# Two modulation sums between two layers: from one f32 product each to two products of rounded type, with the rest made on GpSimd

## The chip, the cores and the metric

The kernel runs on one core of one Trainium2 chip. The metric is the device time of one execution in microseconds. Times in the trace are counted from the start of the profiled span. The engines are TensorE (PE; its weight loads are PEld), VectorE (DVE), ScalarE (ACT), GpSimd (POOL) and SyncE (SP), which issues most of the transfers.

## The reference

256 tokens of width 1024 pass through an attention block with an MLP, then through two layers whose norms are modulated by a vector `c`: layer 0 (convolutions and a recurrent unit, then SwiGLU) and layer 1 (stick-breaking attention, then SwiGLU). All of it is float32. What matters here:

```python
def ada_modulation(c, ada_w, ada_b):
    m = jax.nn.silu(c) @ ada_w + ada_b
    return jnp.split(m, N_MOD, axis=-1)          # sh_m, sc_m, g_m, sh_f, sc_f, g_f

def layer(x, c, ...):                            # both layers have this form
    sh_m, sc_m, g_m, sh_f, sc_f, g_f = ada_modulation(c, ada_w, ada_b)
    h = modulate(rms_norm_2(x, mix_norm), sh_m, sc_m)
    ...
    x = x + g_m[:, None, :] * (o @ w_out)
    hf = modulate(rms_norm_2(x, ffn_norm), sh_f, sc_f)
    return x + g_f[:, None, :] * swiglu(hf, ffn_w_gate, ffn_w_up, ffn_w_down)
```

The changed place is the end of layer 0's SwiGLU, where `g_m` of layer 1 is made ready.

## The kernel before

**Weights in two parts.** Every weight part of 128x1024 is loaded as f32 into `w_raw`, rounded by ScalarE to the type fp32r (`w_hi`, line 728) and its rest `w_raw - w_hi` made by VectorE (`w_lo`, line 1153). Activations are treated alike: `aT_hi` and `aT_lo` are the transposed operand, [128, 8 blocks, 256 tokens] each, `hT_hi` and `hT_lo` the hidden one. A product is then three products of rounded type: hi by hi, hi by lo, lo by hi.

**The modulation.** VectorE accumulates `silu(c) * ada_w` row by row into `mod`, [128, 6 x 1024], so that each partition holds a part of each sum; the count of these steps is `ada_used`. The sum over the partitions is a product with a matrix of ones that leaves the total in every partition of a PSUM bank, and ScalarE copies it back over `mod` (`ada_parts`, line 788, count `ada_out`). A function `ada_sums` does it for 512 columns with one f32 product (line 2165). Four sums of layer 0 are done in another form, `rounded_sums` (lines 2149 and 2150): ScalarE rounds 1024 columns to fp32r in one instruction (`rounded`, line 833, count `ada_hi`), VectorE subtracts to get the rest (`rounded_rest`, line 1376, count `ada_lo`), and TensorE adds ones by hi and ones by lo in one bank, for each 512 columns. `GATE_M` is `mod[:, 2048:3072]`, the columns of `g_m`.

**The place.** After the last down product of layer 0's SwiGLU, TensorE runs `ada_sums(1, 4, 6)` (line 2278), the two sums of `GATE_M` of layer 1. Then comes `entry` (line 1928), the start of layer 1's first projection: eight transposes of token tile 0 (`norm_T`, line 1896), a third sum, ten products of tile 0 with the rounded weights of parts 0 to 3 (line 1942), of which part 3 waits for its rounding by `hi_done`, two more of part 3, four with `aT_lo`, a fourth sum (it waits for `x_ready` of tile 1), the transposes of tile 1, and so on.

What stands around it in the queues, each in program order and with semaphores between them:

- VectorE, `gated_norm` (line 1295): for tile 0 gate times output and residual in two halves (lines 1274 and 1278), times gain (1167); first half of tile 1's gate (1304); times `rstd` plus shift, two halves, which makes `xn` (1178); second half of tile 1's gate, residual of tile 1 (1278), times gain (1167); then `aT_lo` of tile 0 (1161), `xn` of tile 1.
- ScalarE, `norm` (line 756): squares of tile 0 (line 738), a weight rounding, the copies of the two sums, `aT_hi` of tile 0 (777), squares of tile 1, the rounding of weight part 3, and on.
- GpSimd: `row_rstd` (line 643) takes the row sums of the squares (648) and makes `rstd` by a power (649), tile 0 and then tile 1. Before that it fills and loads the biases of layer 1's modulation (638, 639).

The blocks 0 to 3 of `aT_hi` and `aT_lo` are not in use from the last gate and up products of layer 0 until the norm writes them; blocks 4 to 7 hold one weight part there.

Of the kernel before, what the change touches and what calls it, by code (L numbers as in the profile page):

```python
# [26 lines left out]
F32 = mybir.dt.float32  # L27
F32R = mybir.dt.float32r
ALU = mybir.AluOpType
# [8 lines left out]
CH = 512  # L38
# [77 lines left out]
def block_program(nc, a, out):  # L116
    ctx = ExitStack()
    with ctx:
# [19 lines left out]
        aT_hi, aT_lo = aT[:, 0, :, :], aT[:, 1, :, :]  # L138
# [13 lines left out]
        sums = sb("sums", [P, 2])  # L152
# [99 lines left out]
        def flat(h):  # L252
            return h.rearrange("p b n -> p (b n)")
# [19 lines left out]
            return apart[v][1] if v in apart else w_lo[:, slot_of(v), :]  # L273

        hT_sums = flat(hT_hi[:, :, :]), flat(hT_lo[:, :, :])

        def ada_of(j, t):

# [345 lines left out]
        @block.gpsimd  # L624
        def _(pool):
            n_chain = [0]

            def chained(ins):

                n_chain[0] += 1  # L630
                ins.then_inc(pool_chain, 1)
                pool.wait_ge(pool_chain, n_chain[0])

            def start_sums(layer, third, dst=None):

                c = slice(third * UNIT, (third + 1) * UNIT)
                dst = mod[:, c] if dst is None else dst
                chained(pool.memset(dst, 0.0))
                pool.dma_start(dst[0:1, :], ada_b[layer][:, c]).then_inc(ada_bias, 16)

            n_rstd = [0]

            def row_rstd(tiles=(0, 1)):

                for t in tiles:
                    n_rstd[0] += 1
                    pool.wait_ge(sq_done, n_rstd[0])
                    chained(pool.tensor_scalar(var[:, t:t + 1], sums[:, t:t + 1], 1.0 / D, EPS, ALU.mult, ALU.add))
                    pool.tensor_tensor(rstd[:, t:t + 1], var[:, t:t + 1], half[:, 0:1], ALU.pow).then_inc(rstd_done, 1)

            n_half = [0]

            def half_var(t, h):

                n_half[0] += 1
                n_rstd[0] += 1
                pool.wait_ge(sq_half, n_half[0])
                pool.tensor_scalar(var[:, t:t + 1], half_sums[:, 2 * t + h:2 * t + h + 1], EPS, None,
                                   ALU.add).then_inc(var_done, 1)

            pool.memset(eps[:, :], EPS)
            pool.memset(ones[:, :], 1.0).then_inc(consts, 1)
            chained(pool.memset(half[:, :], -0.5))
            chained(pool.memset(ident[:, :], 0.0))
            chained(pool.affine_select(out=ident[:, :], in_=ident[:, :], compare_op=ALU.not_equal, fill=1.0,
                                       base=0, pattern=[[-1, P]], channel_multiplier=1))
            pool.memset(rg_w[:, :, :, :], 0.0).then_inc(consts, 1)
            n_rstd[0] += NT

            chained(pool.iota(neg_dist[:, 0:P], pattern=[[1, P]], base=0, channel_multiplier=-1,  # L670
                              allow_small_or_imprecise_dtypes=True))
            chained(pool.iota(neg_dist[:, P:SC], pattern=[[1, TOK]], base=-P, channel_multiplier=-1,
                              allow_small_or_imprecise_dtypes=True))
            chained(pool.memset(sb_mask[:, :], 0.0))
            pool.affine_select(out=sb_mask[:, :], in_=sb_mask[:, :], compare_op=ALU.is_ge, fill=NEG, base=-1,
                               pattern=[[-1, P]], channel_multiplier=1).then_inc(consts, 1)
            for lo, n, q0 in ((0, P, 0), (P, TOK, P)):
                part = neg_dist[:, lo:lo + n]
                pool.affine_select(out=part, in_=part, compare_op=ALU.is_ge, fill=NEG, base=q0,
                                   pattern=[[-1, n]], channel_multiplier=1).then_inc(consts, 1)  # L680
            for step, n in ATT_STEPS:
                if step == "E" and n < 3:
                    start_sums(0, n)
            pool.wait_ge(o_ready, HEADS)
            pool.wait_ge(mix_used, 11)
            start_sums(1, 0, mod_next)
            half_var(0, 0)
            half_var(1, 0)
            half_var(0, 0)
            half_var(1, 0)  # L690
            half_var(0, 0)
            half_var(0, 0)
            half_var(1, 1)
            half_var(1, 0)
            row_rstd()
            pool.wait_ge(xn_done, 16)
            start_sums(1, 1)
            start_sums(1, 2)
            row_rstd()
            pool.wait_ge(ada_gain_done, 3)  # L700
            chained(pool.memset(stick_new, 0.0))
            for last in (P - 1, SC - 1, SC + P - 1):
                pool.memset(stick_new[:, last:last + 1], 1.0).then_inc(new_sticks, 1)
            row_rstd()
# [3 lines left out]
        def _(act):  # L708
# [47 lines left out]
            def norm(u, layer=None, parts=(0, 0, 0, 0)):  # L756

                k = n_norm[0]
                n_norm[0] += 1
                ada_parts(layer, parts[0], parts[1])  # L760
                for t in range(NT):
                    act.wait_ge(x_ready, 2 * (k - 1) + t + 1)
                    row_square(t, x[:, t, :])
                    if k == 4 or t == 1:
                        split_part(2 * u + 2 + t)
                    ada_parts(layer, parts[1 + t], parts[2 + t])
                    if t == 0:
                        norm_hi(k, 0)
                    if t == 0 and k in (3, 5):
                        split_part(2 * u + 2)  # L770
                norm_hi(k, 1)
# [272 lines left out]
            def swiglu(layer):  # L1044
                u, j0, g0 = SG_U[layer], H0[layer], S0[layer]

                def hi(j, i=None):
                    act.wait_ge(h_ready, plus(j0 + j + 1, i, 2))
                    act.activation(hT_hi[:, hT_blocks(j), :], sg_h, ACT.Copy).then_inc(hT_hi_done, 1)

                def first():

                    split_hi(u + 2)
                    act.wait_ge(w_used, parts_to(u + 2))
                    act.activation(sg_silu, tp[:, :, 0:TOK], ACT.Silu).then_inc(act_h, 1)
                    split_hi(u + 3)
                    act.wait_ge(h_T, 2 + layer)
                    act.activation(hT_hi[:, hT_blocks(0), :], blocks_in(acc[:, 0:1, :])[:, 0],
                                   ACT.Copy).then_inc(hT_hi_done, 1)

                def one(v, j, i=None):

                    if j >= 2:
                        split_part(2 * v + 3, i, 6)
                    split_part(2 * v + 4, i, 6)
                    act.wait_ge(w_used, parts_to(v + 1, i, 6))
                    act.wait_ge(act_h, plus(j0 + j, i, 2))
                    act.activation(sg_gate, ub[:, :, TOK:], ACT.Copy).then_inc(g_rest, 1)
                    split_part(2 * v + 5, i, 6)
                    act.wait_ge(g_sum, plus(g0 + j, i, 2))  # L1070
                    act.wait_ge(h_ready, plus(j0 + j, i, 2))
                    act.activation(sg_silu, sg_gate, ACT.Silu).then_inc(act_h, 1)
                    split_part(2 * v + 6, i, 6)
                    act.wait_ge(w_used, parts_to(v + 2, i, 6))
                    act.activation(sg_up, tp[:, :, TOK:], ACT.Copy).then_inc(u_rest, 1)
                    split_part(2 * v + 7, i, 6)
                    hi(j, i)
                    if i is None and j == NJ_SG - 1:
                        return
                    split_part(2 * v + 8, i, 6)  # L1080

                first()
                one(u + 2, 1)
                with act.Fori(0, (NJ_SG - 3) // 2) as i:
                    for q in range(2):
                        one(u + 5 + 3 * q, 2 + q, i)
                one(u + 3 * NJ_SG - 4, NJ_SG - 1)
                split_hi(u + 3 * NJ_SG)

            swiglu(0)  # L1090
            norm(U_QKV2, 1, (4, 4, 6, 8))

            act.wait_ge(small_loaded, 16 * 8)
# [43 lines left out]
        def _(dve):  # L1137
# [566 lines left out]
                split_lo(u + 3 * NJ_SG)  # L1704

            swiglu(0)
            dve.wait_ge(ada_gain_done, 3)
            gated_norm(3, U_QKV2, gate_ffn, G_M, SH_M)
            ada_gain(1, 4, 20)
# [68 lines left out]
        def _(pe):  # L1778
# [373 lines left out]
            def blocks_of_bank(bank, n):  # L2152
                return bank.rearrange("p (b n) -> p b n", n=n)

            def hT_halves():
                return [[part[:, i * CH:(i + 1) * CH] for i in range(2)] for part in hT_sums]

            def ada_sums(layer, n0, n1):

# [114 lines left out]
                down(u + 3 * NJ_SG - 1, (NJ_SG - 1) % 2, lo_count=j0 + NJ_SG, final=True, left=last_left)  # L2274

            swiglu(0)
            pe.wait_ge(ada_used, 40)
            ada_sums(1, 4, 6)

            def last_sum():  # L2280
                pe.wait_ge(x_ready, 8)
# [98 lines left out]
```

## Time and profile before

| what | us |
|---|---|
| median of 3 runs | 898.9 (898.3 to 899.69) |
| the profiled execution, its own time | 898.97 |
| its span in the trace | 896.9 |
| PE busy | 887.0 (99%) |
| DVE busy | 694.5 (77%) |
| ACT busy | 501.3 (56%) |
| POOL busy | 28.9 (3%) |

The page gives busy time by engine, the chain of work that ended last, and the costliest groups. The timelines list an engine's instructions in order of time, like ones merged, with the idle time before them and what ended it in brackets. The ends of matmuls are modelled: they overlap the next one, so what an instruction takes from the queue is the distance from one start to the next. The profiled execution's own time is 2.07 us more than its span.

### The profile page before, as it was taken

Reading aid. Unit: us, or ns where it says so; the run is one execution under the profiler, and the core shown is the slowest. Engines: PE = TensorE matmul, PEld = TensorE weight load, DVE = VectorE, ACT = ScalarE, POOL = GpSimd, SP = SyncE. Lnnn points to the kernel's source line nnn. Section 1 sums busy time; section 2 is a strip of 40 time slices with the busy share of each in tenths; the row PEclk is TensorE's granted clock in tenths of the full one; section 3 lists DMA queues with packets and bytes.
Section 4 is the critical chain, followed back from the end, with each engine's and each line's share of the span. In section 5 each row is a group of like instructions: output and inputs, shape, how many; then the busy total and the mean of one; then the engine's idle time right before and its main releaser. Section 6 shows DMA issues by size and latency. Waiting matters only on the chain.

```text
span 896.9 us, 13257 instructions
## 1 busy us (share of the span) xinstructions
PE 887.0 (99%) x4833; PEld 749.7 (84%) x4833; DVE 694.5 (77%) x733; ACT 501.3 (56%) x672; POOL 28.9 (3%) x52
## 2 busy tenths in 40 slices
PE   8999999999999999999999999999999999999998
PEld 5998878888888799979888888878777888888886
DVE  4698977998888986996888888686796765655655
ACT  5545675555556758755455455465675465545542
POOL 4000110000000100011000000010000000000000
PEclk9999999999999999999999999999999999999999
DMA  6989586899989375546988888636435366666661
GB/s 219 341 268 350 174 291 205 322 361 354 338 325 329 116 267 179 181 158 205 360 302 319 318 298 282 194 111 211 137 100 150 108 207 192 188 187 187 187 190 67
DMA packets 117091, 208.04 MB, mean 232 GB/s; under 512 B 7236, under 2 KB 81068, under 8 KB 111928
## 3 DMA queue, kind: packets, MB, share of 16 engines
q1 hardware_dynamic: 116566, 205.31, 68.1%
q10 hardware_dynamic: 290, 2.10, 0.7%
q8 instruction: 28, 0.46, 0.2%
q14 instruction: 15, 0.12, 0.0%
q0 software_dynamic: 192, 0.05, 0.0%
HBM read 206.39 MB, written 1.05 MB: 231 GB/s over the span
## 4 chain that ended last, share of the span: by engine, by line
PE 87%; DVE 7%; DMA 2%; ACT 2%; issue 1%; SPq 0%; DVEq 0%; ACTq 0%
PE ub L1923 11%; PE tp L1923 10%; PE acc L1824 7%; PE acc L1825 7%; PE acc L1827 7%; PE ub L1924 5%; PE tp L1924 5%; PE acc L1787 4%; PE acc L1788 4%; PE acc L1789 4%; PE acc L1942 4%; PE tp L1942 3%; PE acc L1910 3%; PE acc L1912 3%; PE acc L1911 3%; DVE w_lo L1153 2%
## 5 line engine op out<-in xcount | busy, mean ns | idle before, releaser
L1153 DVE TENSOR_TENSOR w_lo<-w_raw,w_hi 128x1024 fp32r<-128x1024 f32 x283 | 341.9, 1222 | 109.2 <-ACT w_hi L728 108.7
L728 ACT ACTIVATE w_hi<-w_raw 128x1024 fp32r<-128x1024 f32 x283 | 296.5, 1057 | 216.3 <-PE acc L1827 50.1
L1923 PE MATMUL tp<-aT,w_hi 128*128 128x512 f32 x432 | 153.9, 399 | 0.0
L1923 PE MATMUL ub<-aT,w_hi 128*128 128x512 f32 x432 | 153.6, 398 | 0.0
L1924 PE MATMUL tp<-aT,w_lo 128*128 128x256 f32 x432 | 121.3, 281 | 0.0
L1924 PE MATMUL ub<-aT,w_lo 128*128 128x256 f32 x432 | 121.2, 281 | 0.0
L1824 PE MATMUL acc<-w_hi,hT_hi 128*128 128x512 f32 x284 | 111.5, 393 | 0.7 <-DVE w_lo L1153 0.7
L1825 PE MATMUL acc<-w_lo,hT_hi 128*128 128x512 f32 x284 | 110.6, 390 | 0.0
L1827 PE MATMUL acc<-w_hi,hT_lo 128*128 128x512 f32 x272 | 106.2, 391 | 0.0
L1923 PEld LDWEIGHTS tp<-aT,w_hi 128*128 128x128 f32 x432 | 81.2, 188 | 20.0
L1923 PEld LDWEIGHTS ub<-aT,w_hi 128*128 128x128 f32 x432 | 81.2, 188 | 19.8
L1924 PEld LDWEIGHTS ub<-aT,w_lo 128*128 128x128 f32 x432 | 81.6, 189 | 1.0
L1924 PEld LDWEIGHTS tp<-aT,w_lo 128*128 128x128 f32 x432 | 81.6, 189 | 0.0
L1787 PE MATMUL acc<-w_hi,aT 128*128 128x512 f32 x160 | 64.4, 402 | 0.2 <-DVE aT L1161 0.2
L1824 PEld LDWEIGHTS acc<-w_hi,hT_hi 128*128 128x128 f32 x284 | 53.3, 188 | 12.6 <-DVE w_lo L1153 0.7
L1789 PE MATMUL acc<-w_hi,aT 128*128 128x512 f32 x160 | 62.4, 390 | 0.0
L1788 PE MATMUL acc<-w_lo,aT 128*128 128x512 f32 x160 | 62.4, 390 | 0.0
L1825 PEld LDWEIGHTS acc<-w_lo,hT_hi 128*128 128x128 f32 x284 | 53.4, 188 | 10.4
L1827 PEld LDWEIGHTS acc<-w_hi,hT_lo 128*128 128x128 f32 x272 | 51.0, 188 | 11.4
L1356 DVE SCALAR_TENSOR_TENSOR mod<-ada_raw,silu_c,mod 128x2048 f32<-128x2048 f32 x24 | 56.3, 2345 | 0.2 <-DVE mod L1356 0.2
L1910 PE MATMUL acc<-aT,w_hi 128*128 128x256 f32 x192 | 55.3, 288 | 0.0
L1912 PE MATMUL acc<-aT,w_lo 128*128 128x256 f32 x192 | 54.3, 283 | 0.0
(318 smaller groups left out, 1306.4 us busy)
## 6 DMA issues: line engine op xcount, KB each, us to landing
ada_raw<-in_l_ada_w SPq DMA_DIRECT2D x24, 1024.0 KB, 6.3
w_raw<-in_l_ffn_w_gate SPq DMA_DIRECT2D x44, 512.0 KB, 4.7
w_raw<-in_l_ffn_w_up SPq DMA_DIRECT2D x44, 512.0 KB, 3.8
w_raw<-in_l_ffn_w_down SPq DMA_DIRECT2D x44, 512.0 KB, 3.5
w_raw<-in_w_up SPq DMA_DIRECT2D x32, 512.0 KB, 4.9
w_raw<-in_w_down SPq DMA_DIRECT2D x32, 512.0 KB, 5.7
scratch<-in_l_ada_w SPq DMA_DIRECT2D x14, 1024.0 KB, 7.9
w_raw<-in_attn_w_qkv SPq DMA_DIRECT2D x24, 512.0 KB, 6.2
```

The lines of the kernel that those rows point to most:

```text
L728: act.activation(rounded_part(v), w_raw[:, v % SLOTS, :], ACT.Copy).then_inc(hi_done, 1)
L1153: dve.tensor_tensor(rest_part(v), w_raw[:, v % SLOTS, :], rounded_part(v).bitcast(F32), ALU.subtract).then_inc(lo_done, 1)
L1787: pe.matmul(outp, op_hi[:, k + n, q], wh[:, c], start=start and n == 0, stop=False)
L1788: pe.matmul(outp, op_hi[:, k + n, q], wl[:, c], start=False, stop=False)
L1789: last = pe.matmul(outp, op_lo[:, k + n, q], wh[:, c], start=False, stop=stop and n == 1)
L1824: pe.matmul(outp, operand[0][:, k, q], wh[:, c], start=start, stop=False)
L1825: last = pe.matmul(outp, operand[0][:, k, q], wl[:, c], start=False, stop=False)
L1827: last = pe.matmul(outp, operand[1][:, k, q], wh[:, c], start=False, stop=stop)
L1910: pe.matmul(outp, wh, aT_hi[:, b, :], start=b == 0, stop=False)
L1912: last = pe.matmul(outp, wl, aT_hi[:, b, :], start=False, stop=b == KB - 1)
L1923: pe.matmul(banks[f], rounded_part(v)[:, c], aT[:, :, b, :], start=b == 0, stop=False)
L1924: last = pe.matmul(banks[f][:, 0:TOK], rest_part(v)[:, c], aT_hi[:, b, :], start=False, stop=b == KB - 1)
```

## The change

The two sums of `GATE_M` of layer 1 take the second form. ScalarE rounds `GATE_M` into the blocks 0 to 3 of `aT_hi`, after the last weight rounding of the SwiGLU and ahead of the squares of the next norm; it waits for `ada_used` at 40, which TensorE waited for before. GpSimd, and not VectorE, subtracts for the rest, into the blocks 0 to 3 of `aT_lo`; in its queue that stands between the fills and `row_rstd`. TensorE runs `rounded_sums(16, ...)` in place of `ada_sums(1, 4, 6)` and waits for `ada_lo` at 3. VectorE's part only counts on in the program text. The sums go to the same two banks and are copied by the same instructions.

```diff
@@ -273,6 +273,7 @@
         hT_sums = flat(hT_hi[:, :, :]), flat(hT_lo[:, :, :])
+        aT_sums = flat(aT_hi[:, 0:4, :]), flat(aT_lo[:, 0:4, :])
@@ -696,6 +697,8 @@
             pool.wait_ge(xn_done, 16)
             start_sums(1, 1)
             start_sums(1, 2)
+            pool.wait_ge(ada_hi, 3)
+            pool.tensor_tensor(aT_sums[1], GATE_M, aT_sums[0].bitcast(F32), ALU.subtract).then_inc(ada_lo, 1)
             row_rstd()
@@ -1088,6 +1091,8 @@
             swiglu(0)
+            act.wait_ge(ada_used, 40)
+            rounded(aT_sums, GATE_M)
             norm(U_QKV2, 1, (4, 4, 6, 8))
@@ -1704,6 +1709,7 @@
             swiglu(0)
+            n_rests[0] += 1
             dve.wait_ge(ada_gain_done, 3)
@@ -2152,8 +2158,8 @@
-            def hT_halves():
-                return [[part[:, i * CH:(i + 1) * CH] for i in range(2)] for part in hT_sums]
+            def hT_halves(sums=hT_sums):
+                return [[part[:, i * CH:(i + 1) * CH] for i in range(2)] for part in sums]
@@ -2274,8 +2280,8 @@
             swiglu(0)
-            pe.wait_ge(ada_used, 40)
-            ada_sums(1, 4, 6)
+            pe.wait_ge(ada_out, 16)
+            rounded_sums(16, hT_halves(aT_sums), 3)
```

How the instructions stand on TensorE at the end of the last down product of layer 0 (line 1842) and the start of the entry; a row is a line of the kernel, the operation with the tiles it writes and reads, and what it waits for. First before, then after; the lines of the changed kernel lie a few further on (1896 is 1902, 2165 is 2171, 1942 is 1948):

```order
L1842 MATMUL acc<-aT,hT_lo 128x512
L2165 MATMUL ub<-mod,ones 128x512 [waits ada_out,ada_used]
L2165 MATMUL ub<-mod,ones 128x512 [waits ada_out]
L1896 MATMUL tp<-ident,xn 128x128 [waits xn_done]
L1896 MATMUL tp<-ident,xn 128x128 x3
L1896 MATMUL tp<-ident,xn 128x128 [waits xn_done]
L1896 MATMUL tp<-ident,xn 128x128 x3
L2165 MATMUL acc<-mod,ones 128x512 [waits tile1_gated]
L1942 MATMUL acc<-w_hi,aT 128x512 [waits hi_done,n_hi]
```

```order
L1848 MATMUL acc<-aT,hT_lo 128x512
L2155 MATMUL ub<-aT,ones_r 128x512 [waits ada_lo,ada_out]
L2156 MATMUL ub<-aT,ones_r 128x512
L2155 MATMUL ub<-aT,ones_r 128x512
L2156 MATMUL ub<-aT,ones_r 128x512
L1902 MATMUL tp<-ident,xn 128x128 [waits xn_done]
L1902 MATMUL tp<-ident,xn 128x128 x3
L1902 MATMUL tp<-ident,xn 128x128 [waits xn_done]
L1902 MATMUL tp<-ident,xn 128x128 x3
L2171 MATMUL acc<-mod,ones 128x512 [waits tile1_gated]
L1948 MATMUL acc<-w_hi,aT 128x512 [waits hi_done,n_hi]
```

Two f32 products became four of rounded type, and the wait is for the rests; all behind them stands as before.

GpSimd's queue from the fills of layer 1's biases (638) to the `rstd` of tile 0 of the norm at the changed place, before and after:

```order
L648 TENSOR_SCALAR var<-sums 128x1 [waits sq_done]
L649 TENSOR_TENSOR rstd<-var,half 128x1 [waits pool_chain]
L638 MEMSET mod 128x2048 [waits xn_done]
L639 DMA mod<-in_l_ada_b 1x16x128 [waits pool_chain]
L638 MEMSET mod 128x2048
L639 DMA mod<-in_l_ada_b 1x16x128 [waits pool_chain]
L648 TENSOR_SCALAR var<-sums 128x1 [waits sq_done]
L649 TENSOR_TENSOR rstd<-var,half 128x1 [waits pool_chain]
```

```order
L639 MEMSET mod 128x2048 [waits xn_done]
L640 DMA mod<-in_l_ada_b 1x16x128 [waits pool_chain]
L639 MEMSET mod 128x2048
L640 DMA mod<-in_l_ada_b 1x16x128 [waits pool_chain]
L701 TENSOR_TENSOR aT<-mod,aT 128x1024 [waits ada_hi]
L649 TENSOR_SCALAR var<-sums 128x1 [waits sq_done]
L650 TENSOR_TENSOR rstd<-var,half 128x1 [waits pool_chain]
```

The subtraction (701) stands ahead of the `rstd`, and waits for ScalarE's rounding.

ScalarE's queue from the last hidden rounding of the SwiGLU (1049) to the copies of the two sums (788), before and after:

```order
L1049 ACTIVATE hT_hi<-scratch 128x512 [waits h_ready]
L728 ACTIVATE w_hi<-w_raw 128x1024 [waits w_used,w_loaded2]
L728 ACTIVATE w_hi<-w_raw 128x1024 [waits w_used,w_loaded3]
L738 ACTIVATE scratch,sums<-x 128x1024 [waits x_ready]
L728 ACTIVATE w_hi<-w_raw 128x1024 [waits w_used,w_loaded0]
L788 ACTIVATE mod<-ub 128x512 [waits ada_sum] x2
```

```order
L1052 ACTIVATE hT_hi<-scratch 128x512 [waits h_ready]
L731 ACTIVATE w_hi<-w_raw 128x1024 [waits w_used,w_loaded2]
L731 ACTIVATE w_hi<-w_raw 128x1024 [waits w_used,w_loaded3]
L836 ACTIVATE aT<-mod 128x1024 [waits ada_used]
L741 ACTIVATE scratch,sums<-x 128x1024 [waits x_ready]
L731 ACTIVATE w_hi<-w_raw 128x1024 [waits w_used,w_loaded0]
L791 ACTIVATE mod<-ub 128x512 [waits ada_sum] x2
```

The rounding (836) stands between the weight roundings and the squares of tile 0.

## Rows read from the trace of the kernel before

**Rows 1.** The page, part 1: busy us, share of the span, instructions.

```profile
PE 887.0 (99%) x4833; PEld 749.7 (84%) x4833; DVE 694.5 (77%) x733; ACT 501.3 (56%) x672; POOL 28.9 (3%) x52
```

**Rows 2.** Chain that ended last, 584 to 594 us: start, length, what.

```profile
584.71 1.72 PE ub L2165 x4
```

**Rows 3.** Timeline of PE, 584.2 to 592.9: start, us, line, operation, count.

```profile
584.55 1.88 PE L2165 MATMUL ub<-mod,ones 128*128 128x512 f32 x4
586.27 1.04 PE L1896 MATMUL tp<-ident,xn 128*128 128x128 f32 x8
587.14 1.02 PE L2165 MATMUL acc<-mod,ones 128*128 128x512 f32 x2
...
592.80 0.27 PE L1896 MATMUL ub<-ident,xn 128*128 128x128 f32 x1
```

**Rows 4.** Timeline of PE at the rounded sums of layer 0, from 344.1.

```profile
344.20 0.39 PE L2149 MATMUL tp<-hT_hi,ones_r 128*128 128x512 f32 x1
...
344.89 0.39 PE L2150 MATMUL tp<-hT_lo,ones_r 128*128 128x512 f32 x1
```

**Rows 5.** Timeline of ACT, 576 to 594.

```profile
576.64 2.01 ACT L728 ACTIVATE w_hi<-w_raw 128x1024 fp32r<-128x1024 f32 x2
582.78 1.07 ACT L738 ACTIVATE scratch<-x 128x1024 f32<-128x1024 f32 x1 [4.14 <-DVE x L1278]
583.76 0.18 ACT L738 ACTIVATION_READ_ACCUMULATOR scratch<-x 128x1 f32 x1
...
588.22 1.07 ACT L738 ACTIVATE scratch<-x 128x1024 f32<-128x1024 f32 x1 [0.18 <-DVE x L1278]
...
589.28 1.05 ACT L728 ACTIVATE w_hi<-w_raw 128x1024 fp32r<-128x1024 f32 x1
```

**Rows 6.** Timeline of PE's weight loads, 584.2 to 593.

```profile
590.45 1.23 PEld L1942 LDWEIGHTS acc<-w_hi,aT 128*128 128x128 f32 x6 [0.43 <-issue]
```

**Rows 7.** Timeline of DVE, 577 to 594.

```profile
577.74 2.36 DVE L1153 TENSOR_TENSOR w_lo<-w_raw,w_hi 128x1024 fp32r<-128x1024 f32 x2 [0.15 <-ACT w_hi L728]
...
580.73 0.69 DVE L1278 TENSOR_TENSOR x<-x,xn 128x512 f32<-128x512 f32 x1
...
582.06 0.69 DVE L1278 TENSOR_TENSOR x<-x,xn 128x512 f32<-128x512 f32 x1
582.78 1.22 DVE L1167 TENSOR_TENSOR xn<-x,mod 128x1024 f32<-128x1024 f32 x1
...
584.91 1.41 DVE L1178 SCALAR_TENSOR_TENSOR xn<-xn,rstd,mod 128x512 f32<-128x512 f32 x2 [0.17 <-POOL rstd L649]
...
586.96 1.23 DVE L1278 TENSOR_TENSOR x<-x,xn 128x1024 f32<-128x1024 f32 x1
```

**Rows 8.** Timeline of POOL, 400 to 592.

```profile
404.25 1.83 POOL L638 MEMSET mod<- 128x2048 f32 x1
...
584.04 0.19 POOL L648 TENSOR_SCALAR var<-sums 128x1 f32<-128x1 f32 x1 [177.17 <-ACT scratch L738]
584.31 0.57 POOL L649 TENSOR_TENSOR rstd<-var,half 128x1 f32<-128x1 f32 x1
```

**Rows 9.** Single lines 833 and 1376: duration ns min/median/max, first and last start.

```profile
L833 ACT ACTIVATE hT_hi<-mod x2: 1042/1058/1073, 340.1 to 345.4; 128x1024 fp32r<-128x1024 f32 x2
...
L1376 DVE TENSOR_TENSOR hT_lo<-mod,hT_hi x2: 1219/1222/1226, 341.6 to 346.5; 128x1024 fp32r<-128x1024 f32 x2
```

**Rows 10.** Groups of POOL by shape: count, busy us, mean ns, idle before.

```profile
L679 POOL TENSOR_SCALAR_AFFINE_SELECT neg_dist<-neg_dist 128x256 f32<-128x256 f32 x1 | 0.4, 404 | 0.0
...
L679 POOL TENSOR_SCALAR_AFFINE_SELECT neg_dist<-neg_dist 128x128 f32<-128x128 f32 x1 | 0.3, 291 | 0.0
```

**Rows 11.** Line 658 alone, durations as in rows 9.

```profile
L658 POOL TENSOR_SCALAR var<-half_sums x8: 209/522/2227, 111.2 to 308.1; 128x1 f32<-128x1 f32 x8
```

**Rows 12.** Line 1153 alone, durations as in rows 9.

```profile
L1153 DVE TENSOR_TENSOR w_lo<-w_raw,w_hi x283: 1211/1221/1228, 7.4 to 884.0; 128x1024 fp32r<-128x1024 f32 x142
```

## The prediction

> **What bounds the kernel now.** I read the page first: TensorE (PE) is busy 99% of the span [rows 1], so the first question of any edit is what it takes from TensorE's queue. Then the chain that ended last, in the ten microseconds after layer 0's last down product: it puts the two sums that the change rewrites on the chain, with 1.72 us [rows 2]. Read alone, that row promises the whole of what the sums get cheaper. But the chain only names the engine that was busy; it does not say how far that engine could have moved. So I read, engine by engine, the timelines of the stretch from 577 to 593 us, looking for the places where TensorE meets the others.
>
> There are two. The transposes of tile 0 need `xn`, whose first half VectorE finishes at about 585.66 (half of the pair that starts at 584.91), its second at 586.32 [rows 7]; TensorE comes to them at 586.27 [rows 3], so there it is TensorE that is late. The second place is behind the first ten products of the entry: TensorE's weight load stands at 590.45 after 0.43 us idle [rows 6], put down to "issue". What this product waits for by the code is `hi_done` of part 3 of the weights: ScalarE's rounding that starts at 589.28 and ends at 590.33 [rows 5]. That rounding stands in ScalarE's queue behind the squares of tile 1 (588.22), and these behind VectorE's residual sum of tile 1, which ends at 588.19 (586.96 + 1.23) [rows 5, 7]. So at 590.45 the end is set by the queue of VectorE and not by TensorE, however busy TensorE reads. From 577.74 to that point VectorE's queue has one hole, of 0.17 us before 584.91, and that is a wait for GpSimd's `rstd`, which itself follows from VectorE's own x of tile 0 (582.75) by way of ScalarE and GpSimd [rows 5, 7, 8].
>
> **The change, part by part.** *TensorE.* Removed: two f32 sums of 512 columns. They show as 4 instructions in 1.88 us with the last one's tail; the next instruction starts 586.27 - 584.55 = 1.72 us after the first, 0.43 each [rows 3]. Added: four products of rounded type, the very form that runs for another pair of sums at 344 us: (344.89 - 344.20) / 3 = 0.23 us apart, so 0.92 us [rows 4]. Saving on TensorE: 0.80 us, and they would be through at 585.47.
>
> How much of it gets anywhere: the first four transposes then wait for `xn`, 585.66, and the last four for 586.32. The transposes take 0.87 (587.14 to 586.27) [rows 3], the second four 0.44; with some 0.1 us from a semaphore to a start (0.10 from ScalarE's 583.94 to GpSimd's 584.04 [rows 5, 8]) they end at about 586.9 instead of 587.14. TensorE is then some 0.25 us ahead, with ten products to come before the one at 590.45, and that one is held until ScalarE's 590.33. The lead goes into a longer wait there (0.28 us of real hold now, about 0.5 then). Nothing behind that point moves: the third and fourth sums, the transposes of tile 1 at 592.80 and all that follows keep their places. **Worth of the saving: 0.** If a hole opened in that second wait, at most 0.25 us would pass, and 0.80 us if both did.
>
> *ScalarE.* Added: one rounding of 128x1024, 1.06 us by the same helper's rows [rows 9]. It stands behind the two weight roundings that end at 578.65, and ScalarE is idle from there for 4.14 us, until 582.78 [rows 5]. It ends at 579.71. Its wait, `ada_used` at 40, was met in the loop long before. Queued behind it are only the squares of tile 0 (582.78), so it costs 0; were the cover gone it would cost its 1.06.
>
> *VectorE.* Nothing is added; the line there counts in the program text and issues nothing. *SyncE.* No transfer is added or moved.
>
> *GpSimd.* Added: one subtraction of 128x1024 with two operands from SBUF, from about 579.81. The trace has no such instruction on GpSimd. From below: VectorE does the same in 1.22 us [rows 9]. On GpSimd itself, a pass with one operand costs 291 ns at 128 columns and 404 at 256 [rows 10], so 0.88 ns a column and 0.18 fixed; two operands one after the other make 0.18 + 2 x 0.90 = 1.98 us. From above: the first use of a kind of instruction there took 2227 ns where the shortest of its kind took 209 [rows 11]; 2.02 more makes 4.00. I take 1.98, the row of the same engine: it ends at 581.8 (581.0 to 583.8 over the bounds). The Trainium skill (GPSIMD Engine Reference, section 3.1) has 4497 ns for a `tensor_tensor` of 2048 columns; an estimate of half gives 2.25 us and an end at 582.1, and the sum would be the same.
>
> Two things wait for GpSimd. Behind the subtraction in its queue stands `row_rstd` of tile 0 at 584.04 [rows 8], for which VectorE waits with no slack; and TensorE's sums at 584.55 now wait for `ada_lo`. The slack is 584.04 - 581.80 = 2.24 us, and 0.24 even at the upper bound. So a cost of 0.
>
> The sum: 898.97 (the profiled execution, 0.07 above the median of 898.9) - 0 + 0 = 899.0 us.
>
> **The rivals.** *The two engines get in each other's way.* While GpSimd streams from SBUF, VectorE runs subtractions and additions that also read two SBUF operands: 0.3 us of the last weight rest (to 580.10), the sum at 580.73 (0.69), later the sum at 582.06 and the gain product at 582.78 [rows 7]. VectorE's queue is the one without slack, so what it loses goes into the end one for one. If these run at half speed while GpSimd works, that is 0.30 + 0.69 = 1.0 us later. If GpSimd gives way instead, it gets only the pieces between them, 580.10 to 580.73 and 581.42 to 582.06, 1.27 us, is then shut out until 584.01, ends 0.71 us later at 584.7, and `row_rstd` is late by 0.7. Either way +0.7 to +1.0, about 899.8. For it: both read. Against it: GpSimd's fills of 1.83 us at 404.25 [rows 8] ran across weight rests of VectorE, and all 283 of these lie between 1211 and 1228 ns [rows 12]; but a fill reads nothing. The Trainium skill (GPSIMD Engine Reference, section 8, Key points) says that GpSimd shares its SBUF interfaces with VectorE and collides with VectorE instructions that have two SBUF inputs, which is this rival; no run here shows it for reads.
>
> *GpSimd is late, and the kernel slower.* This is the end on the other side: the subtraction lasts past 584.04, so longer than 4.24 us, and from there each microsecond delays `row_rstd`, `xn` of tile 0 and the whole queue of VectorE by one. It takes a first use that costs more than the 2.02 us seen and shut-out time together: 4.00 + (584.01 - 580.10 - 1.27) = 6.6 us, an end at 586.4, +2.4 us or 901.4. Against it: the short `TENSOR_TENSOR` of `rstd` has run before for the norm of layer 0, so part of the code was used.
>
> *The saving passes.* If the hold at 590.45 is not ScalarE's rounding, 0.25 to 0.80 us arrive, 898.2 to 898.7. Against it: the rounding's end and the hold match to 0.12 us, and the next product needs it by the code.
>
> *The edit doesn't do what it says*, for instance since the sums wait for their rests: then it is 899.0 as well, since TensorE's slack until 590.33 takes up a wait of up to some 1 us (0.80 + 0.28).
>
> **How the numbers follow.** Hidden, no gain (with the last case): 0.52, 899.0. Collision of the engines: 0.33, 899.8. Saving passes: 0.07, 898.5. GpSimd late: 0.08, 901.4. The likeliest case gives 899.0. The range reaches down to the full 0.80 and the spread of the runs before, 897.9, and up to the collision at its dearest plus the same spread, 900.9; it leaves out most of the late GpSimd. A measurement of this kernel tells about 0.2% (1.8 us) from no change. No mechanism of the saving reaches that (0.80 is 0.09%), so faster is only scatter, 0.03; slower is the late GpSimd and the far tail of the collision, 0.10; within, 0.87.
>
> **What the profile after would show.** Right: four products of 0.23 us in place of the sums, transposes of tile 0 up to 0.5 us earlier, a longer hold before the product at 590.45, and the transposes of tile 1 at 592.8 as before; the subtraction on GpSimd ended before 583.8; VectorE's 580.73, 582.06 and 582.78 at 0.69, 0.69 and 1.22. A collision would show as longer ones of these, or as a subtraction over 2.5 us and `row_rstd` after 584.04. Wrong altogether: transposes of tile 1 clearly before 592.8 relative to the last down product.

## The result, and the profile after

The kernel with the change takes 900.09 us (median of 20 runs, 899.36 to 901.01); the kernel before, run beside it, 898.86 us (20 runs, 898.20 to 899.98). The ratio is 1.0013 with a 95% interval of 1.0007 to 1.0019. That is 1.23 us more: inside the range, and within the 0.2% that was called "no change". But the interval does not hold 1, so the kernel is slower by a little over 0.1%, and the likeliest case of the prediction, "hidden, no gain", is not what happened.

Part 1 of the page after answers to [rows 1]:

```profile
PE 887.1 (99%) x4833; PEld 750.8 (84%) x4833; DVE 695.9 (77%) x733; ACT 502.5 (56%) x673; POOL 31.6 (4%) x53
```

The number of TensorE's instructions is the same (the profile showed each f32 product as two), its busy time too. VectorE has the same 733 instructions and is 1.4 us busier: an engine to which nothing was given. That is the first sign of the cause. ScalarE has its one rounding more, GpSimd one instruction of 2.7 us.

The timeline of VectorE after, over the last weight rests, the gated sums of tile 0 and the norm, answers to [rows 7] (start, us, line, operation, count). The profiled run of after reaches this stretch 0.67 us later (578.41 against 577.74 for the same pair of weight rests), from its start on; so durations and distances are to be compared, not starts:

```profile
578.41 2.36 DVE L1158 TENSOR_TENSOR w_lo<-w_raw,w_hi 128x1024 fp32r<-128x1024 f32 x2 [0.15 <-ACT w_hi L731]
580.68 0.68 DVE L1279 TENSOR_TENSOR xn<-acc,gate_ffn 128x512 f32<-128x512 f32 x1
581.40 2.17 DVE L1283 TENSOR_TENSOR x<-x,xn 128x512 f32<-128x512 f32 x1
583.50 0.68 DVE L1279 TENSOR_TENSOR xn<-acc,gate_ffn 128x512 f32<-128x512 f32 x1
584.21 0.69 DVE L1283 TENSOR_TENSOR x<-x,xn 128x512 f32<-128x512 f32 x1
584.94 1.22 DVE L1172 TENSOR_TENSOR xn<-x,mod 128x1024 f32<-128x1024 f32 x1
587.05 1.41 DVE L1183 SCALAR_TENSOR_TENSOR xn<-xn,rstd,mod 128x512 f32<-128x512 f32 x2 [0.17 <-POOL rstd L650]
```

GpSimd's timeline there, as [rows 8]:

```profile
580.36 2.67 POOL L701 TENSOR_TENSOR aT<-mod,aT 128x1024 fp32r<-128x1024 f32 x1 [172.83 <-ACT aT L836]
586.18 0.18 POOL L649 TENSOR_SCALAR var<-sums 128x1 f32<-128x1 f32 x1 [3.16 <-ACT scratch L741]
```

Read the two together. One VectorE row is out of line: the sum `x<-x,xn` at 581.40 takes 2.17 us where the same instruction took 0.69 [rows 7] and takes 0.69 again at 584.21. It is VectorE's first instruction with two SBUF operands after the weight rests. The weight rests end at 578.41 + 2.36 = 580.77, GpSimd's subtraction at 580.36 + 2.67 = 583.03, and the long sum at 583.57, so 0.54 after GpSimd. The product at 580.68, whose one operand is in PSUM (`acc`), takes 0.68 in the midst of it. So the rows read as if the sum did not run slowly but stood until GpSimd was through, and then ran; and as if GpSimd in its turn got going only when the weight rest had ended, so that 583.03 - 580.77 = 2.26 us of its 2.67 are work. Both readings are put to the test below (e4, e5). This is the rival "the two engines get in each other's way", in a harsher form than either of the two that I priced. The Trainium skill (GPSIMD Engine Reference, section 8, Key points) names a contention of GpSimd with VectorE instructions of two SBUF inputs; these rows agree. It also gives 4497 ns for a `tensor_tensor` add of 2048 columns (section 3.1); half of that, 2.25 us, is an estimate for 1024 columns, and the 2.26 agrees.

ScalarE and TensorE, as [rows 5] and [rows 3]:

```profile
579.23 1.04 ACT L836 ACTIVATE aT<-mod 128x1024 fp32r<-128x1024 f32 x1
584.93 1.06 ACT L741 ACTIVATE scratch<-x 128x1024 f32<-128x1024 f32 x1 [4.66 <-DVE x L1283]
```

```profile
585.22 0.40 PE L2155 MATMUL ub<-aT,ones_r 128*128 128x512 f32 x1
585.46 0.40 PE L2156 MATMUL ub<-aT,ones_r 128*128 128x512 f32 x1
585.69 0.39 PE L2155 MATMUL ub<-aT,ones_r 128*128 128x512 f32 x1
585.92 0.40 PE L2156 MATMUL ub<-aT,ones_r 128*128 128x512 f32 x1
587.86 1.32 PE L1902 MATMUL tp<-ident,xn 128*128 128x128 f32 x8 [1.54 <-DVE xn L1183]
```

The rounding is hidden with 4.66 us of idle time behind it, and the four products run 0.23 us apart. But TensorE then waits 1.54 us for the late `xn`, where before it came to the transposes without waiting.

The chain of waits over the same place shows the cause as well, if one looks for a number that is too large rather than for a new name. GpSimd's subtraction is not on it:

```profile
580.68 0.69 DVE xn L1279
581.38 0.02 issue
581.40 2.17 DVE x L1283
```

A measure of the place that does not depend on the start of the run: from the start of the last pair of weight rests to the first transpose of tile 1 ("the site"), and from there to the end of the span. It serves for all that follows.

| kernel | site, us | behind it, us |
|---|---|---|
| before | 15.07 | 304.10 |
| after | 16.52 | 303.79 |

The site is 1.45 us longer, and behind it 0.31 us are gained; the net of 1.14 stands against 1.23 between the medians. Each site below is read from one profiled run, but it repeats well: e1, e4 and e10, in which nothing is held up there, show 15.04 to 15.05, and e2 the 16.52 of after.

### The profile page after: what moved, and what is told of

Read it like the earlier page. It is cut to its first block, busy times and chain, and to the rows that moved or that the text cites. A ratio compares the mean times of both kernels' runs of the same rounds, so it can differ in the third digit from the quotient of the medians.

```text
span 898.7 us, 13259 instructions
## 1 busy us (share of the span) xinstructions
PE 887.1 (99%) x4833; PEld 750.8 (84%) x4833; DVE 695.9 (77%) x733; ACT 502.5 (56%) x673; POOL 31.6 (4%) x53
## 4 chain that ended last, share of the span: by engine, by line
PE 90%; DVE 6%; issue 2%; ACT 1%; DMA 1%; SPq 0%; POOL 0%; DVEq 0%; ACTq 0%
PE ub L1929 11%; PE tp L1929 10%; PE acc L1830 7%; PE acc L1831 7%; PE acc L1833 7%; PE ub L1930 5%; PE tp L1930 5%; PE acc L1793 5%; PE acc L1795 5%; PE acc L1794 5%; PE acc L1948 4%; PE tp L1948 3%; PE acc L1916 3%; PE acc L1918 3%; PE acc L1917 3%
```

## The experiments

The theory after the result: TensorE's saving is taken up by the hold as forecast, and the whole loss is GpSimd's subtraction, which holds up VectorE's instructions with two SBUF operands. The rivals: the sums' new form or TensorE's new wait costs it; VectorE runs at half speed; or anything at all that is added at this place costs the same.

**e1: the sums without the subtraction.** This kernel leaves the rests out of the computation.

```diff
-            pool.wait_ge(ada_hi, 3)
-            pool.tensor_tensor(aT_sums[1], GATE_M, aT_sums[0].bitcast(F32), ALU.subtract).then_inc(ada_lo, 1)
...
-                pe.wait_ge(ada_lo, n)
+                pe.wait_ge(ada_hi if n == 3 else ada_lo, n)
```

> The change without the subtraction on GpSimd: TensorE takes the second product of each sum from what aT_lo held before, so the sums miss their rests (that part of the computation is left out); everything else as in the changed kernel. Measured at the site as the time from the start of the two weight rests of VectorE (577.74 before) to the first transpose of tile 1 (592.80 before): 15.07 us before, 16.52 after. Theory (GpSimd's subtraction locks VectorE out, and the saving on TensorE is absorbed by the hold for ScalarE's weight rounding): 15.07, and the kernel at 1.0000 of before. Rival (the saving passes in part): 14.3 to 14.8, and 0.9991 to 0.9997. Rival (the loss comes from the new products or from ScalarE's rounding): stays near 16.5.

Measured: 898.36 against 898.76 (ratio 0.9996, 0.9987 to 1.0005), site 15.05 us. VectorE's sum is back at 0.69. The weight load behind the first ten products shows where TensorE's 0.80 us went:

```profile
585.17 0.42 PEld L1900 LDWEIGHTS tp<-ident,xn 128*128 128x128 f32 x4 [0.50 <-DVE xn L1181]
...
589.90 1.23 PEld L1946 LDWEIGHTS acc<-w_hi,aT 128*128 128x128 f32 x6 [0.68 <-issue]
```

About 0.5 us are lost again at the transposes, which wait for `xn`: from the first of the sums to the third sum TensorE takes 2.32 us, before 2.59. So 0.27 of the 0.80 are left behind them, and the hold grows from 0.43 [rows 6] to 0.68, by the 0.25 us of the prediction. The whole change without GpSimd's line is worth 0 at this place, as forecast.

**e2: the roundings and the subtraction, but f32 sums.**

```diff
-            pe.wait_ge(ada_out, 16)
-            rounded_sums(16, hT_halves(aT_sums), 3)
+            pe.wait_ge(ada_lo, 3)
+            ada_sums(1, 4, 6)
```

> The two f32 sums of before, with ScalarE's rounding and GpSimd's subtraction of the change kept, though nothing uses their results. Theory (the whole loss is the subtraction on GpSimd at this place): VectorE's first residual sum takes about 2.2 us in place of 0.69, the site 16.5 us, the kernel 1.0013 of before like the changed one. TensorE's transposes of tile 0 wait for xn, so the dearer sums cost nothing. Rival (part of the loss is from the sums of rounded type): clearly under 16.5.

Measured: 900.23 against 898.76 (1.0016, 1.0007 to 1.0025), site 16.52 us as in after.

```profile
580.47 2.17 DVE L1283 TENSOR_TENSOR x<-x,xn 128x512 f32<-128x512 f32 x1
```

So the loss needs nothing of the new sums. With e1, which keeps ScalarE's rounding and is not slower, this leaves only the subtraction.

**e3: the same subtraction on VectorE.**

```diff
-            pool.wait_ge(ada_hi, 3)
-            pool.tensor_tensor(aT_sums[1], GATE_M, aT_sums[0].bitcast(F32), ALU.subtract).then_inc(ada_lo, 1)
...
             swiglu(0)
-            n_rests[0] += 1
+            rounded_rest(aT_sums, GATE_M)
```

> The change with the rest made by VectorE, behind its two weight rests and ahead of the first gate product. Theory (VectorE's queue sets the end here, one for one): the instruction occupies 1.13 to 1.22 us of it, the site is 16.2 us, the kernel about 1.0012 of before, a little better than with GpSimd, though GpSimd was to relieve VectorE. Rival (VectorE has slack here): the site stays at 15.07.

Measured: 899.42 against 898.76 (1.0007, 0.9998 to 1.0016), site 16.19 us.

```profile
580.06 1.22 DVE L1379 TENSOR_TENSOR aT<-mod,aT 128x1024 fp32r<-128x1024 f32 x1
581.20 0.68 DVE L1277 TENSOR_TENSOR xn<-acc,gate_ffn 128x512 f32<-128x512 f32 x1
```

VectorE is 1.14 us later by doing the work itself, and 1.48 us later by "leaving it to GpSimd". At this place the slower engine costs more than it spares: 0.33 us more at the site. The medians alone do not settle that, since the intervals of the two kernels overlap.

**e4: GpSimd's subtraction, some 18 us earlier.** It runs in the SwiGLU of layer 0, where VectorE has gaps. ScalarE rounds into free columns of `scratch`, and GpSimd writes the rest into others beside them. Later ScalarE rounds `GATE_M` again into `aT_hi` and copies the rest into `aT_lo`, and TensorE waits for `ada_hi` at 5 (that line is not shown).

```diff
+                if layer == 0:
+                    act.wait_ge(ada_used, 40)
+                    act.activation(early[0].bitcast(F32R), GATE_M, ACT.Copy).then_inc(ada_hi, 1)
                 one(u + 3 * NJ_SG - 4, NJ_SG - 1)
...
-            act.wait_ge(ada_used, 40)
             rounded(aT_sums, GATE_M)
+            act.wait_ge(ada_lo, 3)
+            act.activation(aT_sums[1], early[1], ACT.Copy).then_inc(ada_hi, 1)
...
-            pool.tensor_tensor(aT_sums[1], GATE_M, aT_sums[0].bitcast(F32), ALU.subtract).then_inc(ada_lo, 1)
+            pool.tensor_tensor(early[1], GATE_M, early[0], ALU.subtract).then_inc(ada_lo, 1)
```

> The subtraction stays on GpSimd, with the same columns and operands from SBUF, but some 20 us earlier, at the start of the last slice of layer 0's SwiGLU (from about 562 us), where VectorE waits for ScalarE for 1.5 us between weight rests; ScalarE rounds there into scratch, GpSimd writes the rest to scratch, and ScalarE brings both into aT in its idle time before the norm. TensorE's sums are those of the change. Theory (what costs is where it runs against VectorE's queue): one weight rest of VectorE or the hole takes it, TensorE waits for nothing, the site is 15.07, the kernel 1.0000 of before (0.9997 to 1.0003). Rival (work on GpSimd, or the sums, cost wherever they stand): 1.0010 or more.

Measured: 898.73 against 898.76 (0.9998, 0.9989 to 1.0008), site 15.05 us. VectorE and GpSimd in the SwiGLU:

```profile
560.43 1.23 DVE L1163 TENSOR_TENSOR w_lo<-w_raw,w_hi 128x1024 fp32r<-128x1024 f32 x1
563.21 1.80 DVE L1163 TENSOR_TENSOR w_lo<-w_raw,w_hi 128x1024 fp32r<-128x1024 f32 x1 [1.55 <-ACT w_hi L732]
566.02 1.23 DVE L1163 TENSOR_TENSOR w_lo<-w_raw,w_hi 128x1024 fp32r<-128x1024 f32 x1 [1.01 <-ACT w_hi L732]
```

```profile
561.43 2.49 POOL L702 TENSOR_TENSOR scratch<-mod,scratch 128x1024 f32<-128x1024 f32 x1 [155.01 <-ACT scratch L1093]
```

The collision is there too, on another line of VectorE and with other tiles, so it hangs neither on one address nor on a semaphore of the changed place. And it follows from the same reading: GpSimd waits for the weight rest that ends at 561.66 and works 2.26 us until 563.92, the same 2.26 although its record is 2.49 long and not 2.67; the rest at 563.21 takes 1.80 instead of 1.22. But of the gap of 1.58 us that stands behind this rest in the kernel before, 1.01 are left, so nobody is late. The same operation costs 1.45 us in a queue without slack and 0 in one with it.

**e5: half of the subtraction (512 columns).** The other half of the rests is left out.

```diff
-            pool.tensor_tensor(aT_sums[1], GATE_M, aT_sums[0].bitcast(F32), ALU.subtract).then_inc(ada_lo, 1)
+            pool.tensor_tensor(aT_sums[1][:, 0:CH], GATE_M[:, 0:CH], aT_sums[0][:, 0:CH].bitcast(F32), ALU.subtract).then_inc(ada_lo, 1)
```

> The change with GpSimd's subtraction cut to its first 512 columns; the rests of the other 512 are left out. So far the subtraction of 1024 columns held VectorE's instruction with two SBUF operands from the end of VectorE's second weight rest until its own end, 2.26 us. Theory (GpSimd holds the way to SBUF for its whole length, in proportion to its columns): it works for 1.13 us, VectorE's first residual sum takes about 1.05 us in place of 2.17 (0.69 undisturbed), the site (from the weight rests to tile 1's transposes) is 15.4 us against 15.07 before and 16.52 after. Rival (a fixed price of the first collision): the residual sum stays near 2.2 and the site near 16.5. Rival (both at half speed, as the prediction had it): the residual sum takes about 1.2 and the second weight rest is longer than 1.22 us.

Measured: site 15.42 us (one run of 899.78 against 898.95).

```profile
578.38 2.36 DVE L1158 TENSOR_TENSOR w_lo<-w_raw,w_hi 128x1024 fp32r<-128x1024 f32 x2 [0.16 <-ACT w_hi L731]
...
581.38 1.07 DVE L1283 TENSOR_TENSOR x<-x,xn 128x512 f32<-128x512 f32 x1
```

```profile
580.33 1.57 POOL L701 TENSOR_TENSOR aT<-mod,aT 128x512 fp32r<-128x512 f32 x1 [172.84 <-ACT aT L836]
```

From the end of the weight rests (580.74) to GpSimd's end (581.90) are 1.16 us, half of 2.26; the sum ends 0.55 after that. The pair of weight rests takes 2.36 us although GpSimd waits beside it for 0.4 us: an instruction that is under way is not slowed. Both speak for "one at a time", against half speed and against a fixed price of the collision.

**e6: two instructions with one operand each in place of the subtraction.** The rests are left out here as well.

```diff
-            pool.tensor_tensor(aT_sums[1], GATE_M, aT_sums[0].bitcast(F32), ALU.subtract).then_inc(ada_lo, 1)
+            pool.tensor_scalar(scratch[:, 8192:9216], GATE_M, 0.0, None, ALU.add)
+            pool.tensor_scalar(aT_sums[1], GATE_M, 0.0, None, ALU.mult).then_inc(ada_lo, 1)
```

> The change with GpSimd's subtraction replaced by two instructions with one SBUF operand each, GATE_M plus 0 into an idle part of scratch and GATE_M times 0 into aT_lo, 1024 columns each, so the rests are left out. The prediction priced one such pass at some 1.08 us, so GpSimd works for about 2 us at the same place. Theory A (only a second SBUF operand on either side collides; one operand on GpSimd goes by): VectorE's residual sum stays 0.69 us and the site 15.07. Theory B (any reading of SBUF by GpSimd holds VectorE's instructions with two SBUF operands): the residual sum takes up to 1.8 us and the site up to 16.2.

Measured: site 16.63 us (one run of 900.46 against 898.95).

```profile
580.73 0.81 DVE L1284 TENSOR_TENSOR x<-x,xn 128x512 f32<-128x512 f32 x1
581.46 0.68 DVE L1280 TENSOR_TENSOR xn<-acc,gate_ffn 128x512 f32<-128x512 f32 x1
582.17 0.69 DVE L1284 TENSOR_TENSOR x<-x,xn 128x512 f32<-128x512 f32 x1
582.90 1.94 DVE L1173 TENSOR_TENSOR xn<-x,mod 128x1024 f32<-128x1024 f32 x1
```

```profile
579.69 3.06 POOL L701 TENSOR_SCALAR scratch<-mod 128x1024 f32<-128x1024 f32 x1 [172.85 <-ACT aT L837]
582.71 2.81 POOL L702 TENSOR_SCALAR aT<-mod 128x1024 fp32r<-128x1024 f32 x1
585.60 0.19 POOL L649 TENSOR_SCALAR var<-sums 128x1 f32<-128x1 f32 x1
```

Neither theory got this. The one-operand form is no quicker than the subtraction, 2.81 to 3.06 us, where from [rows 10] I had estimated about 1.08. And it holds VectorE only in its beginning: the sum at 580.73 loses 0.12, the one at 582.17 nothing although GpSimd's first instruction runs on to 582.75, the product at 582.90 loses 0.72. Counted from VectorE's weight rests (to 580.09) and from GpSimd's second start (582.71), both holds are over after some 0.9 to 1.0 us, by an estimate that lets the held instruction end 0.54 us after the hold for 512 columns, as in after and e5, and 1.09 for 1024, as in e4. The site's +1.56 is about 0.12 + 0.72 + 0.73, the last because `row_rstd` now starts at 585.60, behind GpSimd's own work. The second instruction's length is no slip of the profile: TensorE's first sum waited for it and started at 585.66. If GpSimd waited here too for the VectorE instruction under way, 0.40 us to 580.09 and 0.15 us to 582.86, then both instructions worked 2.66 us. Why they take so long, and why they hold VectorE in their beginning only, stays open; "GpSimd holds VectorE for its whole length" is shown for the subtraction alone.

**e8: a kernel in which the saving gets through.** The hold at [rows 6] depends on VectorE's queue, so I put the subtraction early as in e4, but on VectorE, and moved VectorE's weight rest of part 1 from before the gated sums to behind tile 1's residual sum, with tile 0's `norm_lo` next to it.

```diff
+                if layer == 0:
+                    dve.wait_ge(ada_hi, 3)
+                    dve.tensor_tensor(early[1], GATE_M, early[0], ALU.subtract).then_inc(ada_lo, 1)
                 one(u + 3 * NJ_SG - 4, NJ_SG - 1)
-                split_lo(u + 3 * NJ_SG)
+                if layer == 0:
+                    split_part(2 * (u + 3 * NJ_SG))
+                else:
+                    split_lo(u + 3 * NJ_SG)
...
                 add_gated(1).then_inc(x_ready, 1)
-                dve.wait_ge(x_ready, 2 * n + 2)
-                norm_scale(1, g)
+                split_part(2 * u_end + 1)
                 norm_lo(0, 0)
                 norm_lo(0, 1)
+                dve.wait_ge(x_ready, 2 * n + 2)
+                norm_scale(1, g)
```

> A version that is to beat both. The rest is made early, by VectorE, in its idle 1.5 us between weight rests at about 562 us (rounded into scratch by ScalarE, brought into aT by ScalarE before the norm); and VectorE's queue at the site is shortened where the end hangs on it: the rest of weight part 1 goes from ahead of the first gate product to behind the residual of tile 1, and there the two aT_lo halves of tile 0 go ahead of the gain product of tile 1. Measured from the start of the last down product (584.32 before) to the first transpose of tile 1 (592.80): 8.49 us before, 9.94 after. Theory (the cheaper sums pay only once VectorE's queue is not the limit): 7.7 us, that is 0.8 less than before, the kernel 0.9991 of before. Rival (something else holds the transposes of tile 1): 8.2 or more.

Measured: 897.89 us (897.26 to 898.59) against 898.95; ratio 0.9987, 0.9978 to 0.9996. That is about 0.1% faster than the kernel before; it was not run beside the kernel after, whose ratio to before is 1.0013. From the last down product to the first transpose of tile 1 it takes 7.82 us, before 8.49 and after 9.94.

```profile
586.14 0.68 DVE L1282 TENSOR_TENSOR xn<-acc,gate_ffn 128x512 f32<-128x512 f32 x1
586.86 1.22 DVE L1286 TENSOR_TENSOR x<-x,xn 128x1024 f32<-128x1024 f32 x1
588.00 1.22 DVE L1161 TENSOR_TENSOR w_lo<-w_raw,w_hi 128x1024 fp32r<-128x1024 f32 x1
```

```profile
589.33 0.30 PEld L1958 LDWEIGHTS acc<-w_lo,aT 128*128 128x128 f32 x2 [0.46 <-issue]
...
590.33 1.21 PEld L1958 LDWEIGHTS acc<-w_hi,aT 128*128 128x128 f32 x6 [0.25 <-issue]
```

The hold of [rows 6] has shrunk to 0.25 us, but a new one of 0.46 us stands in front of it. By the code this load waits for the rest of weight part 1, the very instruction that was moved: it ends at 588.00 + 1.22 = 589.22, and the load starts at 589.33. That is why the place takes 7.82 us and not the 7.7 expected.

Of the 1.06 us between the medians, 0.67 us come from the place (8.49 to 7.82). Another 0.32 us lie behind it (303.78 us against 304.10); they come with any added instruction on ScalarE, as e10 shows, and are no merit of the new order.

**e9: the same order of VectorE with the f32 sums of before.** Its edit is the lines of e8 on `split_part`, `norm_lo` and `norm_scale` alone, in the kernel before.

> The kernel before with the new order of VectorE's queue alone, and its two f32 sums. Theory (TensorE then runs without the hold before the product of part 3, but carries the dear sums): only the hold of 0.28 us is gained, 8.2 us from the last down product to the first transpose of tile 1, the kernel 0.9997 of before. The distance to the version with the cheap sums, 0.4 to 0.5 us, is what the change's idea is worth once the queue is moved. Rival (the new order alone brings it all): 7.7 us.

Measured: 898.46 against 898.95 (0.9994, 0.9985 to 1.0003), 8.20 us at the place. The interval holds 1, so the split of e8's gain rests on the two places in the traces: 0.29 us is the order (8.49 to 8.20), and 0.38 us (8.20 to 7.82) the sums of rounded type. So half of TensorE's 0.80 us passes with the new order, and none did with the old. The other half goes mostly to the moved rest: in e9 TensorE, coming later, did not wait for it, and the four products with `w_lo` took 0.91 us; in e8 they take 1.21, and the eight behind them another 0.08 more than in e9.

**e10: one more instruction on ScalarE, of one column, in the kernel before.** This asks for the 0.31 us that after gains behind the site.

```diff
             swiglu(0)
+            act.activation(scratch[:, 8192:8193], eps[:, 0:1], ACT.Copy)
             norm(U_QKV2, 1, (4, 4, 6, 8))
```

> The kernel before with one more instruction on ScalarE, a copy of one column into an idle part of scratch, where the changed kernel has its rounding; nothing reads it. In the profiles so far the time from the first transpose of tile 1 to the end of the span is 304.1 us in the kernel before and in the new order with f32 sums, and 303.8 in all others, and the 0.3 us lie on ScalarE at 693 us, between a wait that is over and the weight rounding behind it (0.33 us against 0.06). Theory (where ScalarE's instructions stand in its stream decides: those two kernels are the only ones without an added instruction on ScalarE): site 15.07 as before, 303.8 behind it, the kernel about 0.9997 of before. Rival (the 0.3 us belong to something else, such as the sums): 304.1.

Measured: behind the site 303.76 us, as in after (303.79), and the site itself 15.04; the time, 898.54 against 898.49 (0.9999, 0.9989 to 1.0008), can't resolve it. The 0.3 us go at one spot, a pair of roundings on ScalarE after a wait; first in the kernel before, then in e10:

```profile
693.49 2.01 ACT L728 ACTIVATE w_hi<-w_raw 128x1024 fp32r<-128x1024 f32 x2 [1.94 <-PE acc L1789]
```

```profile
693.54 2.01 ACT L728 ACTIVATE w_hi<-w_raw 128x1024 fp32r<-128x1024 f32 x2 [1.66 <-PE acc L1790]
```

The wait is 1.94 us before and 1.66 with one instruction more. It is 1.66 in every kernel here that has an added instruction on ScalarE, after among them, and 1.94 in the two that have none, before and e9. So these 0.3 us come with the added instruction and not from anything that the change computes; by what way is not shown.

## Why the prediction was right and wrong, step by step

*TensorE saves 0.80 us, and it is worth nothing.* Right, in size and in place. The products ran 0.23 us apart; e1 showed about 0.5 us going into the wait for `xn` and 0.25 into the hold. The chain [rows 2] had promised a gain of which nothing arrived, and the timelines were right. e8 and e9 confirm it from the other side: with VectorE's order changed, 0.38 us get through. One term stands in the prediction without its working, the 0.28 us of "real hold"; e9, which has no hold there, gained 0.29.

*ScalarE's rounding is hidden.* Right: 1.04 us, with 4.66 us of idle time behind it.

*GpSimd's subtraction takes 1.98 us and costs 0.* This is the step that failed, in two terms. The length, forecast at 1.98 us, was 2.26 us of work (2.67 with the wait for VectorE's weight rest). The row of one operand at 128 and 256 columns [rows 10] was not a sound base for it, as e6 showed later: there one operand of 1024 columns took 2.81 us or more, not 1.08. But 2.26 lay within the bounds of 1.22 and 4.00, and the slack to `row_rstd` covered it: that instruction followed from VectorE's x and never waited for GpSimd. The failure is the 0: I asked only who waits for GpSimd's *result*, and took the slack of those. The one who waits while it works is VectorE, with the next instruction that has two SBUF operands, and VectorE had no slack.

*The chances.* The collision stood among the rivals with 0.33, and "hidden", with 0.52, ahead of it; what happened is the rival. The row against it, the fills of 1.83 us beside undisturbed weight rests [rows 8, 12], was true and no evidence: I had noted myself that a fill reads nothing, and yet let it count.

*The collision's price.* I had 0.7 (GpSimd gives way) and 1.0 (both at half speed). It is neither: whoever has begun finishes, the other stands. VectorE then lost GpSimd's whole 2.26 us less what it could do in the meantime with an operand from PSUM, the product that ended at 581.36. The held sum has its start at 581.40. That leaves 583.03 - 581.40 = 1.63 us of standing, of which 2.17 - 0.69 = 1.48 us shows as a longer sum (it ends 0.54 us after the hold and not 0.69, as if its start had been done by then), and 1.45 us at the site. The rival named the right pair of engines and instructions; its dearest price, 1.0 us, was too small by half a microsecond.

*The sum.* 899.0 was forecast, 900.09 measured. The difference of 1.1 us is +1.45 for the missed term and -0.31 for ScalarE behind the site, which I had not foreseen and which is not owed to the sums.

*The range.* That 900.09 lies inside it is no merit of the likeliest case: the upper end, 900.9, was made for the collision. Some of it is luck, too. The collision cost more than its dearest forecast, and the 0.31 us that nobody foresaw took a part back. The two ends were also not made with "the same spread" as the text says: 898.97 - 0.80 leaves 0.27 us down to 897.9, while 898.97 + 1.0 leaves 0.93 us up to 900.9. With 0.27 on both sides the top would have been 900.2, and the result still inside, by 0.15 us.

## What to carry to other kernels

Before giving an idle GpSimd work with two SBUF operands, look at VectorE's queue at that time and not only at GpSimd's own slack: here the next instruction of VectorE with two SBUF operands stood until GpSimd ended, and all of VectorE's queue behind it. Where VectorE has gaps of that length the work is free (e4), where it has none it costs more than doing it on VectorE (e3). And a saving on a 99% busy engine is worth what the next hold leaves of it: find that hold first, move what it depends on, and then look for the hold that the move has made (e8).

## What the runs showed of the hardware

- A subtraction of two SBUF operands on GpSimd and a subtraction or addition of two SBUF operands on VectorE excluded each other for whole instructions: GpSimd's 1024 f32 columns took 2.26 us in which none of these ran on VectorE, 512 columns 1.16, and GpSimd waited 0.41 us (0.23 in e4) for the VectorE instruction under way. VectorE's product with one operand in PSUM ran beside it at its 0.68 us.
- GpSimd's one-operand instructions of 1024 columns took 2.81 and 3.06 us, longer than the 2.26 of two operands, and held VectorE for an estimated 0.9 to 1.0 us at their start only; a sum of VectorE at 582.17 ran beside the first of them at 0.69 us. Why is not shown.
- One more instruction in ScalarE's program, even of one column, let a later pair of roundings start 0.3 us sooner (idle 1.66 before it, not 1.94). What makes it is open.
